# Order of ScalarE's work inside a step of an attention loop

## The reference

```
A: dilated_attention      4 heads x 3 groups (window, dilation) = (128,1), (512,4), (2048,16)
     s = q.k + bias; m = max(s); p = exp(s - m); denom = sum(p); o = (p / denom) @ v
     the three groups are mixed by softmax of their log-denominators
B: window_gqa_with_sinks  8 query heads on 2 key/value heads, window 128, learned sinks in the denominator
C: forgetting_attention   4 heads, causal over all 512 keys, logit + c_i - c_k (cumulative log gates)
merged = g0*(o_a @ w_a) + g1*(o_b @ w_b) + g2*(o_c @ w_c);   h = merged @ w_out
```

## Time and profile before

| what | value |
|---|---|
| median of three runs | 907.95 us |
| the profiled execution | 909.56 us |
| its span, first to last instruction | 907.8 us |
| TensorE busy | 882.0 us (97%) |
| VectorE busy | 424.1 us (47%) |
| ScalarE busy | 290.8 us (32%) |
| GpSimd busy | 59.0 us (7%) |
| mean granted TensorE clock | 0.997 |
| attention loop in the span | 197.59 to 257.75 us |

### The profile page before, as it was taken

One profiled execution on the slowest core, in us unless ns is written; L12 is line 12 of the kernel. 1 busy time (PEld: TensorE's weight loads), 2 busy tenths in 40 slices (PEclk: granted clock), 3 DMA queues, 4 the chain that ended last, 5 costly groups with the idle time before them and its releaser, 6 DMA issues.

```text
span 907.8 us, 11620 instructions
## 1 busy us (share of the span) xinstructions
PE 882.0 (97%) x4547; PEld 732.8 (81%) x4547; DVE 424.1 (47%) x795; ACT 290.8 (32%) x536; POOL 59.0 (7%) x87
## 2 busy tenths in 40 slices
PE   7999999999999999999999889999999999999996
PEld 7988887777678888888889679888888888888885
DVE  4244347669632525353766784333333333422344
ACT  3112157129642232222424742222222222111221
POOL 2100000080310000000020020000000000000001
PEclk9999999999999999999999999999999999999999
DMA  7524630321002333326515101233322224222321
GB/s 267 158 93 106 151 94 24 113 80 42 2 1 94 106 105 107 98 92 231 191 42 170 57 6 50 93 103 110 106 94 92 92 92 139 93 93 97 109 96 69
DMA packets 70022, 89.88 MB, mean 99 GB/s; under 512 B 2701, under 2 KB 61911, under 8 KB 69983
## 3 DMA queue, kind: packets, MB, share of 16 engines
q1 hardware_dynamic: 69599, 88.92, 30.3%
q0 software_dynamic: 384, 0.43, 0.3%
HBM read 86.81 MB, written 2.52 MB: 98 GB/s over the span
## 4 chain that ended last, share of the span: by engine, by line
PE 91%; ACT 3%; DVE 3%; issue 1%; DMA 1%; POOL 1%; SPq 0%; DVEq 0%; POOLq 0%; ACTq 0%
PE ps L1590 27%; PE ps L1592 27%; PE ps L1591 27%; PE ps L1789 3%; PE ps L1753 2%; PE ps L1718 2%; ACT prob L851 2%; PE ps L1627 1%; DVE w_lo L1083 1%; PE ps L2061 1%; DMA x_nat<-in_x 1%; PE ps L2062 1%; PE ps L2063 1%; ACT w_hi L829 0%; DVE resid L1423 0%
## 5 line engine op out<-in xcount | busy, mean ns | idle before, releaser
L1590 PE MATMUL ps<-xt_hi,w_hi 128*128 128x512 f32 (+1 forms) x712 | 274.6, 386 | 5.6 <-DVE w_lo L1083 2.7
L1591 PE MATMUL ps<-xt_hi,w_lo 128*128 128x512 f32 (+1 forms) x712 | 273.7, 384 | 0.0
L1592 PE MATMUL ps<-xt_lo,w_hi 128*128 128x512 f32 (+1 forms) x712 | 273.6, 384 | 0.0
L1590 PEld LDWEIGHTS ps<-xt_hi,w_hi 128*128 128x128 f32 x712 | 133.8, 188 | 33.8 <-DVE w_lo L1083 3.5
L1591 PEld LDWEIGHTS ps<-xt_hi,w_lo 128*128 128x128 f32 x712 | 133.8, 188 | 26.5
L1592 PEld LDWEIGHTS ps<-xt_lo,w_hi 128*128 128x128 f32 x712 | 133.8, 188 | 26.4
L829 ACT CAST w_hi<-raw 128x1024 fp32r<-128x1024 f32 (+1 forms) x59 | 60.8, 1035 | 184.5 <-PE ps L1592 172.7
L1083 DVE TENSOR_TENSOR w_lo<-raw,w_hi 128x1024 fp32r<-128x1024 f32 (+1 forms) x59 | 71.4, 1213 | 97.6 <-ACT w_hi L829 97.3
L1546 DVE TENSOR_TENSOR w_lo<-raw,w_hi 128x1024 fp32r<-128x1024 f32 x40 | 48.9, 1222 | 79.1 <-ACT w_hi L1042 79.1
L1367 DVE TENSOR_TENSOR w_lo<-raw,w_hi 128x1024 fp32r<-128x1024 f32 x30 | 36.7, 1224 | 91.5 <-ACT w_hi L968 91.5
L1042 ACT CAST w_hi<-raw 128x1024 fp32r<-128x1024 f32 x40 | 41.9, 1047 | 78.8 <-PE ps L1592 78.8
(11 more groups left out here) (254 smaller groups left out, 1275.5 us busy)
## 6 DMA issues: line engine op xcount, KB each, us to landing
raw<-in_w_in SPq DMA_DIRECT2D x24, 1024.0 KB, 5.0
raw<-in_w_ffn_in SPq DMA_DIRECT2D x22, 1024.0 KB, 4.9
raw<-in_w_ffn_out SPq DMA_DIRECT2D x11, 1024.0 KB, 4.8
raw<-in_w_mix_out SPq DMA_DIRECT2D x4, 1024.0 KB, 4.9
x_nat<-in_x SPq DMA_DIRECT2D x4, 512.0 KB, 6.6
raw<-in_w_branch_b SPq DMA_DIRECT2D x4, 512.0 KB, 3.9
resid<-in_x SPq DMA_DIRECT2D x1, 2048.0 KB, 9.6
raw<-in_w_xkv SPq DMA_DIRECT2D x2, 1024.0 KB, 5.1
```

What stands on the lines that cost most here:

```text
L1590: pe.matmul(dst, a_hi, b_hi, start=start, stop=False)
L1591: pe.matmul(dst, a_lo, b_hi, start=False, stop=False)
L1592: return pe.matmul(dst, a_hi, b_lo, start=False, stop=stop)
```

## The change

In ScalarE's list, three pieces of a step change places. Before, `first_part` (step 2, 4, 6, 8) and `recip_copy` stood between the step's drain and its exponentials; now the exponentials come right behind the drain, then the copy of reciprocals, then the first part. No instruction is added or removed, no wait is changed, and the lists of the other engines stay as they are.

```diff
             for i in range(N_GROUP_PAIRS):
                 if i + 1 < N_GROUP_PAIRS:
                     pt_drain(2 * i + 2)
+                if i == 0:
+                    split(PG + 1)
+                for j, b in SIDE[i - 1] if i else []:
+                    exps(j, b)
+                if i in RECIP_AT:
+                    recip_copy(N_AH + RECIP_AT.index(i))
                 if i - 1 in out_end[:N_AH]:
                     first_part(out_end.index(i - 1))
-                if i == 0:
-                    split(PG + 1)
-                if i in RECIP_AT:
-                    recip_copy(N_AH + RECIP_AT.index(i))
-                for j, b in SIDE[i - 1] if i else []:
-                    exps(j, b)
```

## The result

The changed kernel takes 911.19 us (median of 22 runs, 909.18 to 912.61), the kernel before beside it 909.01 us (median of 22, 906.07 to 911.50; this median is higher than the 907.95 of the first three runs). The ratio is 1.0021, with a 95% interval of 1.0013 to 1.0029: slower by 1.9 us, between 1.2 and 2.6. The prediction was plus 2.9, so the direction is right and the size too large by more than the interval allows.

What follows compares the result with a forecast made beforehand. TensorE, 97% busy, was taken as the bound, with three engines nearly full early in the loop. Plus 3.65 us for four out_drain waits, minus 0.77 in step 17, gave 907.95 + 2.9 = 910.8 us; range 908.0 to 912.2.

Steps and rivals of the forecast that it cites:

- The gain in step 17: Step 17: exponentials start at the drain's end instead of after the copy of reciprocals, so TensorE resumes 0.77 us earlier.
- The first wait: Step 2: out_drain(0) waits for the moved first_part(0) and starts 0.83 us late, making TensorE as late from step 4.
- The closed chain: Steps 2 to 8: out_drain to next out_drain through VectorE and ScalarE takes 6.61 us per two steps, 5.48 before.
- That nothing else moves: Later copies of reciprocals end before their users need them, and behind the loop the lateness stays.
- The sum: Whole kernel: plus 3.65 us for four out_drain waits, minus 0.77 in step 17, plus 2.9 us.
- Rival 1: Steps 2 to 8: VectorE absorbs out_drain's wait, only step 17 counts; 907.2 us, chance 0.08.
- Rival 2: Steps 2 to 8: only the first wait counts, later ones are covered; 908.0 us, chance 0.14.
- Rival 3: Loss without the gain: step 9's copy of reciprocals late too, or step 17's scores last; 911.6 us, chance 0.13.

Runs made afterwards that it cites:

- first_only: Against the kernel before, only the first parts moved behind the exponentials, copies of reciprocals left in front; loop 63.43 us against 60.16, ratio 1.0051.
- recip_only: Against the kernel before, only the copies of reciprocals (all six) moved behind the exponentials; loop 59.27 us against 60.16, ratio 0.9989.
- half_way: Against the kernel before, first part behind two of the four exponentials in steps 2, 4, 6, 8, copies of reciprocals in front; loop 60.49 us, ratio 0.9998.
- recip_only_again: The kernel of recip_only measured once more beside the unchanged kernel before; loop 59.27 us against 60.16, ratio 1.0000.
- recip_step17: Against the kernel before, only the copy of reciprocals of step 17 moved behind the exponentials; loop 59.27 us against 60.16, ratio 1.0011.

## Why the prediction was right, and where its size was off

- **The gain in step 17** was put at 0.77 us and is 0.88 in the changed kernel, 0.89 alone. The step that was mis-sized is the start of the exponentials. I let them start at the drain's end; in fact the next instruction starts 0.27 us behind the start of a drain of 0.37. I took the reported duration for what an instruction costs, in a place where no start of a follower was to be had.
- **The first wait** was put at 0.83 us; `out_drain(0)` is 0.76 us late, counted from the start of the loop (10.51 against 9.75 us). It is the same error once more: `first_part(0)` was let start at the end of the last accumulator read, 0.19 us behind its start, and starts 0.09 behind it (206.00 against 205.91 in the profile after). The other way, `first_part` and its signal take 0.67 us, not 0.63.
- **The closed chain** was put at 6.61 us for two steps, three times 19.83; it is 6.54, 6.39 and 6.54, together 19.47. The mis-sized terms: the drain was read as 0.48 us in step 4 and costs 0.36 in each of the three turns. The kernel before had both values in its own trace, 0.48 in steps 4 and 8 and 0.38 and 0.37 in steps 2 and 6; what makes the difference no run shows. The exponentials of the even step took 0.13 us less in the second turn (1.76), and `first_part` with its signal 0.04 to 0.06 more in each. So `out_drain(3)` is 3.80 us late, not 4.23, and TensorE 3.29, not 3.65. That is most of the error of the whole.
- **That nothing else moves**: right. The other copies of reciprocals are free, and behind the loop the delay stays: 649.87 us from its end to the end of the span, 650.05 before (the span is given to 0.1 us).
- **The sum** was plus 2.9 us; the loop has plus 2.41, the times 1.9 (1.2 to 2.6). first_only and recip_only add up to it: 3.27 less 0.89 is 2.38. That the forecast of 910.8 us lies so near the measured 911.19 is in part luck: it was added to 907.95, and the kernel before measured 909.01 over 22 runs, from which the same sum gives 911.9.
- **Rival 1** (swallowed) is out: with the first parts alone moved TensorE is 3.27 us late (first_only). The 0.2 us that VectorE can give back in two steps is too small against turns that are 0.7 to 0.9 us longer than TensorE's 5.67. The Trainium skill, "Perfetto Trace Analysis", section "Identifying the Most-Contended Engine", says to optimize the engine with the highest occupancy first. Who takes from it that the order on a less busy engine is no matter is misled here: ScalarE was third by busy time in the window from 203 us and second in the one from 218 us, and the order of its list alone made 3.27 us on TensorE. Nor was ScalarE near full in the first of these windows, as the prediction has it against this rival: 76%, with TensorE and VectorE above 99%. **Rival 2** (only the first wait counts) is out: one wait is 0.77 us, four are 3.27. **Rival 3** (loss without gain) is out: the gain is 0.88 us with the whole loss in front of it and 0.89 without.

## What to carry to other kernels

Before an instruction is moved on one engine, follow who waits for it and what stands behind that waiting instruction; if that leads back to the first engine, add up the turn and compare it with what the busiest engine needs for the same stretch. Turns about as long as that are nearly free even with waits in them (half_way: 5.66, 5.69 and 5.95 us against 5.67), and each turn that is longer costs the difference again. A wait that does not come back is a plain delay, and costs what the slack behind it does not cover (0.77 us in step 2, 1.22 in step 8). And a change of two moves is better read as two: here one of them, in one step, gains 0.89 us of loop, and the other loses 3.27.

## What the runs showed beside it

In the twelve profiles, executions differ outside the loop, in two stretches that none of these kernels touches: the loop starts between 195.03 and 197.59 us, and the part behind it takes 649.87 to 653.21 us. These ranges are 2.6 and 3.3 us wide, and single runs of one kernel are spread over 5 us. At the start, TensorE waits for the input: its second transposes start at 7.96 us in the profile before and at 7.14 in the one after. Its first products take 0.41 us each, and 0.28 from about 15.0 us on before, from about 12.0 us on after, while the granted clock of these windows reads 1.00 throughout; why they are slow at first no run shows. The first of 0.28 us behind the third transposes starts 1.40 us earlier in the profile after, which is all but 0.03 of the 1.43 us. Behind the loop, two windows of two kernels, the columns as in the earlier trace rows (the number behind the last count is the granted clock of TensorE, 1.00 for 2.4 GHz), first the kernel before, with 650.05 us behind the loop:

```profile
470.00:530.00 60.00, 55.40 (x375) 46.82 (x373) 42.11 (x107) 31.75 (x71) 4.59 (x7) 0.97 0.26 88
530.00:560.00 30.00, 27.04 (x215) 26.08 (x215) 18.40 (x27) 11.05 (x17) 5.46 (x6) 1.00 0.11 36
```

then recip_only_again, with 653.21:

```profile
470.00:530.00 60.00, 54.67 (x365) 45.76 (x363) 41.41 (x107) 29.91 (x67) 4.04 (x7) 0.94 0.27 88
530.00:560.00 30.00, 27.52 (x207) 26.73 (x208) 17.76 (x27) 11.04 (x17) 4.82 (x6) 0.94 0.11 36
```

These are the cross attention and the layer norms around it, where TensorE has gaps. In all twelve profiles the part behind the loop is 649.87 to 650.28 us where the two numbers are 0.97 and 1.00, 650.64 to 650.95 (recip_step17: 651.24) where one is 0.94 and the other 1.00 in either order, 651.70 with 0.97 and 0.94, and 652.56 and 653.21 with 0.94 twice. In windows of 1 us of recip_only_again the granted clock is below 1.00 from 510 to 517 us, and 0.50, which is 1.2 GHz, from 511 to 516; TensorE was busy for 0.63 us of the 2 us before. In the kernel before it is below 1.00 from 512 to 516 us and 0.50 from 513 to 515, again behind 2 us with 0.63 us busy. In the kernel before, the runs with a mean granted clock of 0.994 or less took 1.9 to 2.4 us longer on average than the others (three series of 29 runs). So a granted clock that dips for some microseconds where TensorE has gaps is worth more than the whole change, and it differs from execution to execution of one kernel. What decides when it dips no run here shows.
